# Attention in a two-block network kernel: exponentials ahead of the projection's read-out on ScalarE, the second half of softmax ahead of the joint norms on VectorE, and those norms sooner in layer two

## The chip, the cores and the metric

The kernel runs on one core of a Trainium2 chip. The metric is the device time of one execution in microseconds; the time before is the median of three runs. Five engines work side by side, each through its own list of instructions, in order: TensorE (PE, matrix products and transposes into the eight PSUM banks), VectorE (DVE), ScalarE (ACT), GpSimd (POOL) and SyncE (SP, which issues the weight loads). They are tied together by semaphores written out by hand.

## The reference, cut to what matters

The reference is a two-layer block (attention, spatial gating, a Fourier mixer and a squared-ReLU MLP over 256 latent and 256 context tokens, width 1024) followed by a second block (a gated recurrence, gated linear attention and a mixture of 32 experts). The change touches the attention of the first block alone, of the context in layer one (`context_attention`) and of the latents in both layers (`latent_window_attention`):

```python
s = einsum(q, k) * hd ** -0.5              # 8 heads, 2 kv heads; latents see 256 own + 256 context keys
p = softmax(concatenate([s, s_sink]))      # a learned sink score per head joins each row
out = einsum(p, v)
...
def merge_heads(attn, sgu, four, g_mix, w_out):
    a = rmsnorm(attn, g_mix[:ATTN_WIDTH])                            # "mA"
    s = rmsnorm(sgu, g_mix[ATTN_WIDTH:ATTN_WIDTH + SGU_WIDTH])       # "mS"
    f = rmsnorm(four, g_mix[ATTN_WIDTH + SGU_WIDTH:])                # "mF"
    return jnp.concatenate([a, s, f], axis=-1) @ w_out
```

The three norms of `merge_heads` are the joint norms of this document: mF (Fourier part), mS (gating part) and mA (attention part). Nothing that is computed changes; only the order does.

## The kernel before, in words

X names the latent stream and C the context stream; features lie on partitions and 256 tokens along the free axis. A projection step i (0 to 11) is `w_in(l, s, i)` on TensorE, 16 matmul instructions, and `projected(l, s, i)` on ScalarE, which copies the bank out; steps 6 to 9 go through a GELU, which needs another table of functions than the exponential, so the table is loaded before the GELU and `log_exp()` loads the other one back.

Attention is cut into 8 units: unit u is one pair of heads (one of each kv head, "halves" hf 0 and 1) and one block of 128 queries. A unit runs through these stages:

- `scores` (TensorE, line 572): two products into two neighbouring banks.
- `soft_a` (VectorE, lines 1923 to 1929): for X the band mask, then the maximum, the sink, and the negated maximum, which releases the exponentials (`s_mx`, line 1927).
- `exponentials` (ScalarE, lines 1384 and 1387): two exponentials from the score banks to SBUF, each of which releases its bank, and the sink's.
- `soft_b` (VectorE, lines 1936 to 1940): the sum, its reciprocal, and two products with it, each of which releases (`s_pn`) the transposes of its half.
- `turned` (TensorE, line 580): transposes of the probabilities into two banks. `read_outs` (ScalarE, line 1291) copies those of unit u and the output of unit u-1 out.
- `values` (TensorE, line 594): the product with the values.

TensorE's loop iteration `attention(l, s, i)` issues scores(i+1), turned(i-1) and values(i-2). In layer one the context's attention rides on the latents' projection: step i of it issues `w_in(0, X, i)` and then `attention(0, C, i-2)`. In the latents' attention the filler is pieces of the context's `w_out` (layer one) and rows of the modulation `ada` / `ada_turn` (both layers).

A joint norm goes through all engines: squares on ScalarE, their sum on GpSimd (line 2550), a product with a constant matrix on TensorE (`merge`, that is `mean_summed`, line 478), `mean_read` on VectorE (line 1833), `root` on ScalarE (a logarithm and an exponential, lines 1324 and 1326), `refined` on VectorE (three operations, lines 1838 to 1840) and `scaled` on VectorE (line 1948, one operation per block of 128 features). `value_norm` on VectorE with `value_roots` on ScalarE (lines 1362, 1364) normalises the gating's values before `gating` (line 554).

PSUM banks are handed out in turn by `Fills.take` in the order in which TensorE's code asks; a taker waits until the bank's last user has freed it. So moving one `merge` shifts the bank of everything behind it. The weights go through a ring of three buffers that SyncE refills; in the expert stage it has eight.

Of the kernel before, what the change touches and what calls it, by code (L numbers as in the profile page):

```python
# [14 lines left out]
X, C = 0, 1  # L15
# [102 lines left out]
def build(nc, A, out):  # L118
    (T1, W1), (T2, W2) = smalls()
    ctx = ExitStack()  # L120
    with ctx:
# [299 lines left out]
        def _(pe):  # L421
# [407 lines left out]
            pe.wait_ge(s_kz, 4)  # L829
            scores(1, X, 0)  # L830
            for i in range(10):
                if i == 3:
                    merge("mF", 1, X)
                if i == 5:
                    merge("mS", 1, X)
                attention(1, X, i)
                if 1 <= i <= 4:
                    ada_turn(1, 5 + i)
                if i <= 3:
                    ada(1, 6 + i)  # L840
# [430 lines left out]
        def _(act):  # L1271
# [7 lines left out]
            def freed(key):  # L1279
                b, n, m = F.at[key]  # L1280
                act.wait_ge(s_free[b], n)
# [39 lines left out]
            def root(key, s=0, slot=0):  # L1321

                freed(("ms",) + key)
                S.up(act.activation(stat(s, slot), HOLD[:, 256 * s:256 * s + 256], ACT.Ln))
                act.wait_ge(s_act, S.n)
                act.activation(stat(s, slot), stat(s, slot), ACT.Exp, scale=-0.5).then_inc(s_root, 1)

            def log_exp():
                act.preload_act_table_set("natural_log_exp_and_others")
# [10 lines left out]
            def projected(l, s, i):  # L1340
                key = ("in", l, s, i)
                ks = slice(256 * s, 256 * s + 256)
                if i < 4:
                    evac(Q[s][:, i, :], key)
                elif i == 4 and s == X:
                    evac(KR, key)
                elif i == 4:
                    b = full(key)
                    act.activation(KZ[0:64, 0, ks], banks[b][0:64, 0:256], ACT.Copy)
                    act.activation(KZ[64:128, 1, ks], banks[b][64:128, 0:256], ACT.Copy).then_inc(s_free[b], 1)  # L1350
                elif i == 5:
                    evac(V[:, 2 * s:2 * s + 2, :].rearrange("p a b -> p (a b)"), key)
                elif i < 8:
                    evac(U[s][:, i - 6, :], key, ACT.Gelu_apprx_tanh)
                elif i < 10:
                    evac(GV[s][:, i - 8, :], key, ACT.Gelu_apprx_tanh)
                else:
                    evac(FT[s][:, i - 10, :], key)

            def value_roots(l, s):  # L1360
                act.wait_ge(s_vss, MIX[l, s] + 1)
                S.up(act.activation(SV[:, 32:40], SV[:, 16:24], ACT.Ln))
                act.wait_ge(s_act, S.n)
                act.activation(SV[:, 48:56], SV[:, 32:40], ACT.Exp, scale=-0.5).then_inc(s_vrt, 1)
# [9 lines left out]
            def exponentials(l, s, i):  # L1374
                wd = 512 if s == X else 256
                if i < 8:
                    u, par = units(l, s) + i, i % 2
                    mx, dn, es, nm = (v[:, 2 * par:2 * par + 2] for v in (MX, DN, ES, NM))
                    act.wait_ge(s_mx, u + 1)
                    if i >= 2:  # L1380
                        full(("t", l, s, i - 2, 1))
                    for hf in range(2):
                        b = full(("s", l, s, i, hf))
                        act.activation(P[:, par, hf, 0:wd], banks[b][:, 0:wd], ACT.Exp, bias=mx[:, hf:hf + 1], scale=0.125,
                                       accum_out=dn[:, hf:hf + 1]).then_inc(s_free[b], 1)
                    act.wait_ge(s_es, u + 1)
                    act.activation(es, nm, ACT.Exp).then_inc(s_ex, 1)
# [72 lines left out]
            for i in range(12):  # L1460
# [7 lines left out]
                if i == 9:  # L1468
                    log_exp()
            for i in range(12):  # L1470
                projected(0, X, i)
                if 6 <= i <= 9:
                    log_exp()
                if i == 0:
                    fourier_d(0, C)
                if i == 1:
                    fourier_t(0, C)
                    merge_squares("mF", 0, C)
                    merge_squares("mS", 0, C)
                if i >= 2:  # L1480
                    exponentials(0, C, i - 2)
                if i == 5:
                    root(("mF", 0, C), C, 0)
                if i == 7:
                    root(("mS", 0, C), C, 1)
                if i >= 2:
                    read_outs(0, C, i - 2)
            value_roots(0, X)
            fourier_d(0, X)
            merge_squares("mA", 0, C)  # L1490
            fourier_t(0, X)
# [74 lines left out]
            for i in range(10):  # L1566
                exponentials(1, X, i)
                if 1 <= i <= 4:
                    row(1, 5 + i)
                if i == 3:  # L1570
                    root(("mF", 1, X), X, 0)
                if i == 5:
                    root(("mS", 1, X), X, 1)
                read_outs(1, X, i)
            merge_squares("mA", 1, X)
# [220 lines left out]
        def _(dve):  # L1796
# [18 lines left out]
            def turned(l, c):  # L1815
                b = full(("turn", l, c))
                part = banks[b][:, :].rearrange("p (j g s) -> p j g s", j=4, g=4)
                sums = MODT[:, 192:200].rearrange("p (j s) -> p j s", s=2)
                bias = s1(f"b_ada{l}")[:, 4 * c:4 * c + 4].rearrange("p (j o) -> p j o", o=1).broadcast_to([128, 4, 2])
                if ADA[l, c]:  # L1820
                    dve.wait_ge(s_mod, ADA[l, c])
                dve.tensor_reduce(sums, part[:, :, :, 0:2].rearrange("p j g s -> p j s g"), AX.X, ALU.add).then_inc(s_free[b], 1)
                freed(("turn", l, c))
                dve.tensor_tensor(mod(l)[:, 4 * c:4 * c + 4, :], sums, bias, ALU.add).then_inc(s_mod, 1)
# [6 lines left out]
            def mean_read(key, eps, s=0):  # L1831
                b = full(("ms",) + key)
                dve.tensor_scalar(HOLD[:, 256 * s:256 * s + 256], banks[b][:, 0:256], eps, None, ALU.add).then_inc(s_free[b], 1)  # L1833

            def refined(key, s=0, slot=0):
                r, me, tm = stat(s, slot), HOLD[:, 256 * s:256 * s + 256], HOLD[:, 512 + 256 * s:768 + 256 * s]
                dve.wait_ge(s_root, ROOT[key] + 1)
                step(dve.tensor_tensor(tm, r, r, ALU.mult))
                step(dve.scalar_tensor_tensor(tm, tm, -0.5, me, ALU.mult, ALU.mult))
                step(dve.scalar_tensor_tensor(r, tm, 1.5, r, ALU.add, ALU.mult))  # L1840
                return r
# [259 lines left out]
            for i in range(10):  # L2101
                if i < 8:
                    soft_a(0, X, i)
                if i == 0:
                    mean_read(("mA", 0, C), 1e-6, C)
                if i == 1:
                    refined(("mA", 0, C), C, 2)
                    scaled("mA", 0, C, (0, 1))
                if i == 2:
                    scaled("mA", 0, C, (2, 3))  # L2110
                if 2 <= i <= 3:
                    turned(0, 8 + i)
                if i == 4:
                    gain(0, 3, 5, "g_post_ff", 0.0)
                if i == 3:
                    mean_read(("mF", 0, X), 1e-6, X)
                if i == 4:
                    refined(("mF", 0, X), X, 0)
                if i == 5:
                    scaled("mF", 0, X)  # L2120
                    mean_read(("mS", 0, X), 1e-6, X)
                if i == 6:
                    refined(("mS", 0, X), X, 1)
                if i == 7:
                    scaled("mS", 0, X)
                if 1 <= i < 9:
                    soft_b(0, X, i - 1)
            merge("mA", 0, X)
            post("mix", 0, C)
# [33 lines left out]
            for i in range(10):  # L2163
                if i < 8:
                    soft_a(1, X, i)
                if 2 <= i <= 5:
                    turned(1, 4 + i)
                if i == 3:
                    mean_read(("mF", 1, X), 1e-6, X)
                if i == 4:  # L2170
                    refined(("mF", 1, X), X, 0)
                if i == 5:
                    scaled("mF", 1, X)
                    mean_read(("mS", 1, X), 1e-6, X)
                if i == 6:
                    refined(("mS", 1, X), X, 1)
                if i == 7:
                    scaled("mS", 1, X)
                if 1 <= i < 9:
                    soft_b(1, X, i - 1)  # L2180
            gain(1, 1, 2, "g_post_mix", 0.0)
            gain(1, 2, 4, "g_pre_ff", 1.0)
            merge("mA", 1, X)
# [637 lines left out]
```

## Time and profile before

| | |
|---|---|
| median of three runs | 2383.97 us (2383.86 to 2388.11) |
| profiled execution, its own time | 2384.43 us |
| its span in the trace | 2382.6 us |
| TensorE busy | 2286.0 us, 96% |
| VectorE busy | 811.3 us, 34% |
| ScalarE busy | 489.6 us, 21% |
| GpSimd busy | 145.7 us, 6% |
| layer one: context attention inside the latents' projection | 110 to 180 us |
| layer one: latents' attention | 180 to 240 us |
| layer two: latents' attention | 764 to 811 us |
| expert stage, DMA engines full | from about 1490 us |

A line of the timeline gives the start, how long the group took, the engine, the line of the kernel, the operation, what it writes and reads with shapes, how many instructions were merged, and in brackets how long the engine stood idle just before and what released it. Idle time of TensorE is what counts here; the time of another engine matters only where TensorE waits for it.

### The profile page before, as it was taken

The page shows a single profiled execution, that of the slowest core. Times are in us where ns is not written, and L with a number is a line of the kernel's source. Part 1 is how long each engine was busy: PE and PEld are TensorE (multiplying, and loading weights), DVE is VectorE, ACT ScalarE, POOL GpSimd, SP SyncE. Part 2 cuts the span into 40 slices and gives each one's busy share as a digit, 9 for nine tenths or more (in the row PEclk, how much of TensorE's full clock was granted, in tenths as well). Part 3 has the DMA queues.
Part 4 walks back from the last instruction along what each step waited for, and adds up shares of the span by engine and source line. Part 5 has one row for each costly group of instructions (what it writes and reads, how often), then busy time and mean ns, then how long its engine had stood idle before and what let it go on. Part 6 is the DMA issues. An engine that isn't in the chain of part 4 may idle for free.

```text
span 2382.6 us, 34249 instructions
## 1 busy us (share of the span) xinstructions
PE 2286.0 (96%) x14400; PEld 1672.6 (70%) x14400; DVE 811.3 (34%) x2062; ACT 489.6 (21%) x1153; POOL 145.7 (6%) x150
## 2 busy tenths in 40 slices
PE   6989999999999999999999989999999999999998
PEld 4766888888887678887698855555555555555556
DVE  2245454578434420004674322222222222212224
ACT  3255410000023432101543210111111111111113
POOL 1000211144301000000000000000000000000000
PEclk9999999999999999999999989999999999999999
DMA  8722212134233344345333757999999999999993
GB/s 362 279 106 107 106 71 106 71 129 155 107 141 124 137 172 169 141 145 203 118 131 114 295 235 273 428 426 427 427 426 427 426 426 426 427 427 426 427 426 130
DMA packets 42262, 601.61 MB, mean 252 GB/s; under 512 B 4689, under 2 KB 5329, under 8 KB 5745
## 3 DMA queue, kind: packets, MB, share of 16 engines
q1 hardware_dynamic: 41616, 593.30, 61.4%
q10 hardware_dynamic: 480, 5.97, 0.6%
q8 instruction: 121, 1.98, 0.3%
q14 instruction: 45, 0.36, 0.0%
HBM read 598.20 MB, written 1.05 MB: 252 GB/s over the span
## 4 chain that ended last, share of the span: by engine, by line
PE 85%; DMA 10%; DVE 2%; ACT 2%; issue 1%; POOL 0%; SPq 0%; POOLq 0%; DVEq 0%; PEldq 0%; ACTq 0%
PE PS L1112 15%; PE PS L1136 8%; PE PS L866 8%; PE PS L641 7%; PE PS L676 6%; DMA RG<-in_w_up 6%; PE PS L625 6%; PE PS L728 5%; PE PS L516 4%; PE PS L615 3%; DMA BIG<-in_w_up 3%; PE PS L714 2%; PE PS L1041 2%; PE PS L1148 2%; PE PS L456 1%; PE PS L1107 1%
## 5 line engine op out<-in xcount | busy, mean ns | idle before, releaser
L2410 DVE TENSOR_SCALAR STAT<-PS 128x128 f32<-128x128 f32 (+1 forms) x128 | 37.8, 295 | 669.7 <-PE PS L1112 669.7
L1112 PE MATMUL PS<-BIG,XS 128*64 128x256 f32 (+1 forms) x2016 | 238.8, 388 | 3.3 <-DMA BIG<-in_w_up 3.3
L1112 PEld LDWEIGHTS PS<-BIG,XS 128*64 128x64 f32 (+1 forms) x2016 | 146.5, 139 | 93.8 <-issue 21.4
L1291 ACT ACTIVATE BIG<-PS 128x256 f32<-128x256 f32 (+2 forms) x205 | 85.7, 430 | 499.6 <-PE PS L641 138.9
L1112 PE MATMUL PS<-RG,XS 128*64 128x256 f32 (+1 forms) x1520 | 178.5, 385 | 5.3 <-DMA RG<-in_w_up 5.3
L866 PE MATMUL PS<-XS,RG 128*128 128x256 f32 x768 | 172.8, 383 | 5.0 <-DVE XS L1867 4.1
L866 PEld LDWEIGHTS PS<-XS,RG 128*128 128x128 f32 x768 | 146.3, 192 | 26.7 <-issue 6.9
L1112 PEld LDWEIGHTS PS<-RG,XS 128*64 128x64 f32 (+1 forms) x1520 | 108.3, 138 | 73.7 <-issue 15.6
L1716 ACT ACTIVATE STAT<-STAT 128x128 f32<-128x128 f32 (+1 forms) x128 | 40.1, 313 | 572.8 <-DVE STAT L2410 572.8
L1833 DVE TENSOR_SCALAR HOLD<-PS 128x256 f32<-128x256 f32 x27 | 11.4, 422 | 401.6 <-PE PS L492 301.4
L625 PE MATMUL PS<-HN,RG 128*128 128x256 f32 x640 | 142.0, 385 | 4.0 <-ACT HN L1338 4.0
L625 PEld LDWEIGHTS PS<-HN,RG 128*128 128x128 f32 x640 | 123.5, 193 | 22.0 <-issue 4.6
L1136 PE MATMUL PS<-BIG,CAT 128*64 128x256 f32 (+1 forms) x992 | 121.3, 388 | 0.8 <-DMA BIG<-in_w_down 0.7
L728 PE MATMUL PS<-BIG,RG 128*128 128x256 f32 x512 | 110.7, 379 | 0.0
L516 PE MATMUL PS<-HN,RG 128*128 128x256 f32 x448 | 103.0, 386 | 5.7 <-ACT HN L1338 5.7
L728 PEld LDWEIGHTS PS<-BIG,RG 128*128 128x128 f32 x512 | 97.3, 190 | 13.2
L1136 PEld LDWEIGHTS PS<-BIG,CAT 128*64 128x64 f32 (+1 forms) x992 | 73.4, 139 | 43.8 <-issue 10.0
L516 PEld LDWEIGHTS PS<-HN,RG 128*128 128x128 f32 x448 | 85.1, 193 | 21.6 <-issue 10.0
L2550 POOL TENSOR_TENSOR HN<-HN 128x256 f32<-128x256 f32 x72 | 54.7, 760 | 671.4 <-ACT HN L1319 248.6
L615 PE MATMUL PS<-CAT,RG 128*128 128x256 f32 x384 | 87.1, 386 | 0.2 <-DVE CAT L1948 0.2
L1136 PE MATMUL PS<-RG,CAT 128*64 128x256 f32 x768 | 86.4, 381 | 0.4 <-DVE CAT L2419 0.4
L615 PEld LDWEIGHTS PS<-CAT,RG 128*128 128x128 f32 x384 | 73.2, 192 | 11.7 <-issue 1.0
(353 smaller groups left out, 3286.0 us busy)
## 6 DMA issues: line engine op xcount, KB each, us to landing
BIG<-in_w_up SPq DMA_DIRECT2D x64, 2048.0 KB, 27.1
RG<-in_w_up SPq DMA_DIRECT2D x48, 2048.0 KB, 27.9
RG<-in_w_ff SPq DMA_DIRECT2D x32, 2048.0 KB, 7.7
BIG<-in_w_down SPq DMA_DIRECT2D x32, 2048.0 KB, 29.3
RG<-in_w_ada SPq DMA_DIRECT2D x24, 2048.0 KB, 7.9
RG<-in_w_down SPq DMA_DIRECT2D x24, 2048.0 KB, 28.7
RG<-in_w_in SPq DMA_DIRECT2D x23, 2048.0 KB, 7.9
SM<-in_w_up SPq DMA_DIRECT2D x16, 2048.0 KB, 27.4
```

Source lines behind the costliest of these rows:

```text
L516: m = pe.matmul(banks[b][:, 0:256], w[:, k, c0:c0 + 128], N[:, k, :], start=k == 0, stop=k == 7)
L615: m = pe.matmul(banks[b][:, 0:256], w[:, k, 128 * (n % 4):128 * (n % 4) + 128], own(CAT, s)[:, k, :], start=i == 0, stop=i == 7)
L625: m = pe.matmul(banks[b][:, 0:256], w[:, k, 128 * n:128 * n + 128], own(HN, s)[:, k, :], start=k == 0, stop=k == 7)
L641: m = pe.matmul(banks[b][:, 0:256], w[:, k, :], a[:, k, :], start=not first and k == 0, stop=k == 3, skip_group_check=True)
L676: return pe.matmul(banks[b[j]][:, 256 * half:256 * half + 256], w, a, start=first and half == 0, stop=last, skip_group_check=True)
L714: m = pe.matmul(banks[b[s, o]][:, 0:256], w[:, k, 128 * o:128 * o + 128], own(FFH, s)[:, 16 * h + k, :], start=h + k == 0, stop=h * 16 + k ...
L728: m = pe.matmul(banks[b][:, 0:256], w[:, k, :], own(FFH, s)[:, k, :], start=k == 0, stop=k == 31)
L866: m = pe.matmul(banks[b][:, 0:256], w[:, k, 128 * n:128 * n + 128], src[:, k, 0:256], start=k == 0, stop=k == 7)
L1112: i = pe.matmul(half_of(b, h, sides), Xg[:, k, 0:cap], w[:, k, h * wd:h * wd + wd], start=False, stop=k == 7)
L1136: m = pe.matmul(half_of(b, h, sides), T_[:, k, :], w[:, k, h * wd:h * wd + wd], start=k == 0, stop=k == 7)
L1291: i = act.activation(dst, banks[b][rows, part], fn)
L2550: S.up(pool.tensor_tensor(H[:, i, :], H[:, i, :], H[:, k, :], ALU.add))
```

## The change

Three edits, in four engine programs' order of instructions; none is added or removed.

- ScalarE, layer one, projection of X with the attention of C: in step i the exponentials of unit i-2 come before the projection's read-out and not after it; the root of mF moves from step 5 to step 6 and that of mS from step 7 to step 8, each right behind the exponentials; `value_roots` comes before the read-out of step 11; the reload of the exponential's table moves from right behind the GELU to the end of the step, behind the read-outs.
- VectorE, layer one, attention of X: soft_b of unit 0 comes before `refined` and `scaled` of mA in iteration 1.
- Layer two, attention of X: on TensorE `merge` of mF and mS moves from iterations 3 and 5 to 1 and 2, and with it `root` on ScalarE. On VectorE soft_b comes right behind soft_a, ahead of all norm work, and that moves up: mean_read of mF to iteration 1, refined mF and mean_read mS to 2, refined mS to 3, the two `scaled` to 4 and 5.

```diff
@@ tensor, layer two
             for i in range(10):
-                if i == 3:
+                if i == 1:
                     merge("mF", 1, X)
-                if i == 5:
+                if i == 2:
                     merge("mS", 1, X)
                 attention(1, X, i)
@@ scalar, layer one
             for i in range(12):
+                if i >= 2:
+                    exponentials(0, C, i - 2)
+                if i == 6:
+                    root(("mF", 0, C), C, 0)
+                if i == 8:
+                    root(("mS", 0, C), C, 1)
+                if i == 11:
+                    value_roots(0, X)
                 projected(0, X, i)
-                if 6 <= i <= 9:
-                    log_exp()
                 if i == 0:
                     fourier_d(0, C)
...
                 if i >= 2:
-                    exponentials(0, C, i - 2)
-                if i == 5:
-                    root(("mF", 0, C), C, 0)
-                if i == 7:
-                    root(("mS", 0, C), C, 1)
-                if i >= 2:
                     read_outs(0, C, i - 2)
-            value_roots(0, X)
+                if 6 <= i <= 9:
+                    log_exp()
@@ scalar, layer two
                 exponentials(1, X, i)
...
-                if i == 3:
+                if i == 1:
                     root(("mF", 1, X), X, 0)
-                if i == 5:
+                if i == 2:
                     root(("mS", 1, X), X, 1)
@@ vector, layer one, attention of X
                 if i == 1:
+                    soft_b(0, X, 0)
                     refined(("mA", 0, C), C, 2)
                     scaled("mA", 0, C, (0, 1))
...
-                if 1 <= i < 9:
+                if 2 <= i < 9:
                     soft_b(0, X, i - 1)
@@ vector, layer two, attention of X
             for i in range(10):
                 if i < 8:
                     soft_a(1, X, i)
+                if 1 <= i < 9:
+                    soft_b(1, X, i - 1)
                 if 2 <= i <= 5:
                     turned(1, 4 + i)
+                if i == 1:
+                    mean_read(("mF", 1, X), 1e-6, X)
+                if i == 2:
+                    refined(("mF", 1, X), X, 0)
+                    mean_read(("mS", 1, X), 1e-6, X)
                 if i == 3:
-                    mean_read(("mF", 1, X), 1e-6, X)
+                    refined(("mS", 1, X), X, 1)
                 if i == 4:
-                    refined(("mF", 1, X), X, 0)
+                    scaled("mF", 1, X)
                 if i == 5:
-                    scaled("mF", 1, X)
-                    mean_read(("mS", 1, X), 1e-6, X)
-                if i == 6:
-                    refined(("mS", 1, X), X, 1)
-                if i == 7:
                     scaled("mS", 1, X)
-                if 1 <= i < 9:
-                    soft_b(1, X, i - 1)
```

## Rows read from the trace of the kernel before

**Rows 1.** The page: busy share of the DMA engines in 40 slices of 59.6 us.

```profile
DMA  8722212134233344345333757999999999999993
```

**Rows 2.** Waits of TensorE from 95 to 260 us (total, times, longest).

```profile
PE PS L580 <- ACT BIG L1384: 3.0, 2, 1.5
PE PS L572 <- ACT BIG L1384: 2.2, 2, 2.0
PE PS L594 <- ACT BIG L1384: 1.9, 1, 1.9
```

**Rows 3.** Timeline of TensorE, layer one, projection of X.

```profile
139.93 0.90 PE L580 MATMUL PS<-SM,BIG 128*128 128x128 f32 x4 [1.49 <-ACT BIG L1384]
...
163.71 3.72 PE L516 MATMUL PS<-HN,RG 128*128 128x256 f32 x16
...
175.46 1.09 PE L554 MATMUL PS<-SM,BIG 128*64 128x128 f32 x16 [0.85 <-DVE BIG L1900]
```

**Rows 4.** Timeline of ScalarE, the same stretch.

```profile
131.90 0.42 ACT L1324 ACTIVATE STAT<-HOLD 128x256 f32<-128x256 f32 x1
...
134.27 1.28 ACT L1291 ACT_TABLE_LOAD   x1
...
138.01 1.28 ACT L1329 ACT_TABLE_LOAD   x1
139.31 0.47 ACT L1384 ACTIVATE BIG<-PS,MISC 128x256 f32<-128x256 f32 x1
```

**Rows 5.** Timeline of VectorE, the same stretch.

```profile
135.30 0.17 DVE L1927 TENSOR_SCALAR MISC<-MISC 128x2 f32<-128x2 f32 x1
...
135.59 0.42 DVE L1838 TENSOR_TENSOR HOLD<-STAT 128x256 f32<-128x256 f32 x1
...
137.35 0.62 DVE L1940 TENSOR_SCALAR BIG<-BIG,MISC 128x256 f32<-128x256 f32 x2
```

**Rows 6.** Timeline of VectorE, layer one, attention of X.

```profile
186.75 0.42 DVE L1838 TENSOR_TENSOR HOLD<-STAT 128x256 f32<-128x256 f32 x1
...
189.30 0.88 DVE L1940 TENSOR_SCALAR BIG<-BIG,MISC 128x512 f32<-128x512 f32 x2
...
193.78 0.88 DVE L1940 TENSOR_SCALAR BIG<-BIG,MISC 128x512 f32<-128x512 f32 x2
```

**Rows 7.** Timeline of TensorE, the same stretch.

```profile
189.94 1.06 PE L580 MATMUL PS<-SM,BIG 128*128 128x128 f32 x8 [1.66 <-DVE BIG L1940]
...
195.04 1.04 PE L580 MATMUL PS<-SM,BIG 128*128 128x128 f32 x8
```

**Rows 8.** Waits of TensorE from 690 to 860 us.

```profile
PE PS L580 <- DVE BIG L1940: 2.8, 2, 2.1
```

**Rows 9.** Timeline of VectorE, layer two, end of the attention of X.

```profile
797.67 0.42 DVE L1838 TENSOR_TENSOR HOLD<-STAT 128x256 f32<-128x256 f32 x1
...
799.04 0.16 DVE L1936 TENSOR_TENSOR MISC<-MISC 128x2 f32<-128x2 f32 x1
...
800.24 0.42 DVE L1923 TENSOR_TENSOR PS<-PS,SM 128x256 f32<-128x256 f32 x1
...
802.43 0.87 DVE L1948 SCALAR_TENSOR_TENSOR CAT<-CAT,SM,STAT 128x256 f32<-128x256 f32 x2
```

**Rows 10.** Timeline of TensorE, layer two, attention of X.

```profile
764.54 3.70 PE L572 MATMUL PS<-BIG 128*128 128x512 f32 x8
768.17 1.92 PE L456 MATMUL PS<-RG,SM 128*32 128x512 f32 x16
...
804.24 1.59 PE L580 MATMUL PS<-SM,BIG 128*128 128x128 f32 x8 [2.08 <-DVE BIG L1940]
...
813.62 0.67 PE L478 MATMUL PS<-HN,MISC 128*128 128x256 f32 x2 [2.78 <-POOLq L2553]
```

**Rows 11.** Stretches of TensorE: length, busy (instructions), granted clock, DMA share, GB/s.

```profile
804.00:808.00 4.00, 3.76 (x26) 0.58 0.00 0
859.60:866.40 6.80, 6.53 (x16) 0.52 0.19 82
```

## The prediction, written before the changed kernel was run

> **What bounds the kernel now.** I read the page first. TensorE is busy for 96% of the span, so only its idle time, and time at the lower clock, can be won. In the last third the DMA engines are full [rows 1], but that stage begins when the stages before it have freed their buffers, and TensorE's program gets there in order; so what is won ahead of it should shift it whole. Then the waits of TensorE in the two stretches that the diff touches. From 95 to 260 us three groups wait for line 1384, ScalarE's exponentials, 7.1 us together [rows 2]; in the timeline they are one wait of 1.5 to 2.0 us in each of steps 6 to 9 of the projection, two of them ahead of transposes [rows 3]. Why there: ScalarE's list puts the exponentials behind the step's read-out, that waits for the end of a projection on TensorE, and from step 6 on a table load of 1.28 us follows, and only then the exponentials [rows 4]. The scores' maximum had been there since 135.47 [rows 5], so they come 3.8 us late (139.31), and the transposes' banks are those that they free. Behind it `gating` waits 0.85 us for VectorE's value norm [rows 3], which stood behind `value_roots`.
>
> In the latents' attention of layer one there is one wait, 1.66 us [rows 7]: the first transposes, for a soft_b that stands behind `refined` and `scaled` of mA [rows 6]. In layer two two waits, 2.8 us, for soft_b [rows 8]; the larger stands at 804.24 and behind it TensorE ran near half clock, 1.2 of 2.4 GHz, until 808 [rows 10, 11]. There VectorE is the bound: an iteration costs it 2.2 for soft_a and 1.2 for soft_b (800.24 to 802.43, 799.04 to 800.24) and 0.8 to 1.4 for a piece of a norm (797.67 to 799.04, and line 1948) [rows 9], some 4.4 to 4.8, against 3.9 of TensorE (scores 1.85, half of 3.70 [rows 10], transposes 1.0 [rows 7], values some 1.0). In iterations 0 to 3 the modulation adds over 1.9 to TensorE [rows 10], and VectorE has slack.
>
> **The change, part one: layer one's projection.** Steps 2 to 5 gain next to nothing (0.1), as no wait stands there. I name the steps by their transposes.
>
> Step 6: exponentials at 135.5 and not 139.3; two at 0.47 and the sink's take some 1.1. But the root of mF now stands behind them on ScalarE (0.42 and 0.42 [rows 4], so it ends at 137.45) while `refined` kept its place on VectorE, ahead of soft_b: queued behind the later root are `refined`, soft_b and the transposes. From the start of `refined` to the start of line 1940 is 1.76 [rows 5], its first half some 0.37 and the semaphore some 0.15: 139.74, against 139.93 before. The wait changes hands; with the second half of the transposes, 0.4 won.
>
> Step 7: ScalarE copies out, loads the exponential's table (1.28) and runs the exponentials from 142.6; both banks are free at 143.7, and TensorE, 0.4 earlier, asks at 144.9. The 2.0 us wait goes. Next late is soft_b behind mean_read of mS, 0.4 to 0.5. In all 2.1 won so far.
>
> Step 8 is as step 6, with mS. From the transposes of step 7 (146.35) on: copies out until 147.9, table 1.28, exponentials 1.1, root 0.85, `refined` and soft_b 2.3: 153.4, against 155.63 before. TensorE is there at 152.0 and waits 1.4; 2.4 won so far.
>
> Step 9 has no root: soft_b is done by 156.5, TensorE comes at 158.2, and the bank for the values (scores of unit 7) is free at 156.8. The 1.9 us wait goes whole, and step 10's product starts at 159.3, not 163.71 [rows 3]: 4.4 won. `value_roots` now stands at 164.5, as the squares' sums are there by 161, and the value norm is ready when `gating` asks: 0.9. **Part one: -5.3 us** (7.9 of idle and some 0.6 inside the stretched rows go, 3.2 come back). The GELU's read-outs are now later by up to 1.3, behind a table load, and cover is there: their banks are asked for a step later, some 2 us at least. Bounds: nothing of steps 6 and 8, -4.4; no new wait at all, -8.5.
>
> On the table loads the rows show the next instruction right behind: 138.01 plus 1.28 and the exponential starts at 139.31 [rows 4]. The Trainium skill (ScalarE: Activation LUTs, What ACT_TABLE_LOAD costs) adds a drain of 1380 ns to each switch, 2.66 us in all. The trace does not agree for this kernel; by the page the load of step 7's end, which lies on the path to step 8's transposes, would cost 1.4 more, and with it the sum about 1.4 to 2.8 less.
>
> **Part two: layer one's latents.** soft_b of unit 0 now starts at 186.75, where `refined` stood; it needs some 1.0 to the first release, so 187.8, and TensorE arrives at 188.2. The 1.66 go. But VectorE's work up to soft_b of unit 1 is the same in sum, and its line 1940 stays at 193.78 [rows 6]: with 0.48 for a half and the semaphore, transposes at 194.4, which TensorE could have had at 193.3. Against 195.04 [rows 7] **-0.6 us** is left; behind it TensorE has no wait and all follows it. Bounds: 0 and -1.7.
>
> **Part three: layer two.** `merge` of mF and mS on TensorE is the same some 0.4 each, sooner; GpSimd's sums for both are there before iteration 1. VectorE does the norms in iterations 1 to 5, of which 1 to 3 have slack; in 6 and 7 it has 3.4 against 3.9. What is late next is the tail: unit 7's soft_a can start only when its scores end, and soft_a and soft_b to the first release of unit 6 take 2.2 and 1.0 and 0.15, some 3.4, while TensorE has 2.0 (transposes and values): 1.4 of wait. Gone are 2.8 and 0.2 of wait, 0.2 in stretched rows and half of the 3.76 us at half clock, 1.9 [rows 8, 11]. **-3.7 us.** The 2.78 us behind the last values [rows 10] stay: squares, GpSimd, product. Bounds: if VectorE's backlog only moves, -1; no wait at all, -5.1.
>
> The moved merges shift the banks: scores of units 3, 4 and 5 now take the banks of the scores before them, so a new wait on the exponentials is possible. Unit 3 asks for its second bank at 776.9; the exponentials of unit 2, which have the root of mF and the copies of unit 0's transposes ahead of them, free it at 776.3. Cover 0.6; without it the cost is what is missing, one to one.
>
> Sum: -5.3 - 0.6 - 3.7 = **-9.6 us**. The profiled execution took 2384.43, 0.46 above the median of 2383.97; against the median the forecast is **2374.4 us**.
>
> **The rivals.** (a) *VectorE stays the bound in layer two.* For: it ran without a gap before 804. Against: the count above, 3.4 against 3.9. It would give -1 in place of -3.7, 2377.1. Chance 0.11.
>
> (b) *The clock falls elsewhere.* A fall can take 6.8 us at half rate (859.60 on [rows 11]), 3.4 us lost, and such places stand in the old kernel behind idle TensorE. With the tail's wait still there and the eight matmuls behind it done sooner at full clock, more idle follows in a short time, and a fall could come when work is not waiting anyway: +1.7 to +3.4, 2376.1 to 2377.8. Against: waits of 2.0 and 1.5 us, 7 us apart in layer one, brought no fall. Chance 0.08. By the Trainium skill (TensorE: Matmul & The Clock Gate, What's actually happening) the throttled clock is the default and activity releases it; rows 11 fit that.
>
> (c) *A table load costs more in its new place.* Before, loads followed a copy; now the GELU's follows the exponentials directly and the exponential's a copy. If a switch there held ScalarE for twice its 1.28 [rows 4], the paths to the transposes of steps 7 and 8 would be 1.3 longer each: 2.6 less gain, 2377.0. Against: the exponential in rows 4 starts 0.02 behind its load. Chance 0.03. By the page named above (ScalarE: Activation LUTs, of the Trainium skill) it would be 1.4 each.
>
> (d) *The change does little.* If the new order only swaps the waited-for engine: steps 6 to 8 and layer two keep their waits, only step 9 and gating are won, and 1.9 and 0.9 and 0.6 are left: 2380.6; if the shift is swallowed by weight loads in the DMA-bound stage, 2384. Chance 0.08, mostly within 0.2%.
>
> (e) *Slower: the shifted banks.* If ScalarE's list holds the exponentials of units 2, 3 and 4 behind root and copies for longer than the 0.6 of cover, scores of 3, 4 and 5 wait each. At the price of the worst old wait, 2.1, with a clock fall of 1.7 behind each, that is 11.4, and the old 3.7 are not won: -5.9 + 11.4 = +5.5, 2389.5. It decides when the exponentials of unit 2 end over 0.6 us later than I have them. Against: ScalarE has a quarter of the load there. Chance 0.04.
>
> **How the numbers follow.** The forecast's own case has 0.66 and spans -8 to -12. A measurement of this kernel can tell about 0.2%, 4.8 us, from no change. Forecast, (a), (b) and (c) are all faster by more than that: 0.88. Within 0.2%: 0.08 from (d). Slower: 0.04. The range for 8 in 10 is 2370.8 (step waits smaller than counted, no further fall of the clock) to 2379.0 (bounds of parts one and three at their weak end).
>
> **What would show it.** In the changed profile TensorE's waits for line 1384 in 130 to 165 us should be gone, and two waits of 1.3 to 1.4 us for line 1940 should stand at 138.4 and 152.0, right behind ScalarE's roots; the product of step 10 at about 159.3; no wait ahead of `gating`; the first transposes of the latents without a wait and a new one of about 1 us ahead of the second; in layer two one wait of 1.4 us some 4 us before the last values, no stretch at 0.50 clock ahead of them, and the last `merge` about 9.6 us sooner. A wait of scores (line 572) for line 1384 near layer two's third iteration would show (e) at work. The forecast is wrong if the last `merge` has moved by 9 or more and the total by under 7: then the later stages took it back.

## The result, and the profile after

| | before | changed |
|---|---|---|
| median of five runs each | 2383.86 us (2380.69 to 2388.11) | 2370.30 us (2369.08 to 2372.89) |
| span of the profiled execution | 2382.6 us | 2368.4 us |
| TensorE busy | 2286.0 us | 2277.5 us |

The ratio is 0.9938 (95% interval 0.9922 to 0.9955): times 2383.86 that is 14.8 us less, between 10.7 and 18.6; the medians differ by 13.6. The forecast was 9.6 us less, and the median lies half a microsecond below its range. Faster was right; the size was not, and the question for the experiments is where the other 4 us come from.

First the waits of TensorE in the changed kernel, two lines from 95 to 260 us and two from 690 to 830 us (total, times, longest), against [rows 2, 8]:

```profile
PE PS L580 <- DVE BIG L1941: 4.4, 5, 1.3
PE PS L492 <- ACT HN L1401: 0.5, 1, 0.5
...
PE PS L615 <- DVE CAT L1949: 1.6, 1, 1.6
...
PE PS L580 <- DVE BIG L1941: 1.4, 1, 1.4
```

No wait for line 1384, the exponentials, is left; what remains waits for soft_b (line 1941, one line down from 1940). TensorE's timeline of layer one's projection and of the latents' first steps answers to [rows 3, 7]:

```profile
131.02 0.67 PE L580 MATMUL PS<-SM,BIG 128*128 128x128 f32 x4 [0.40 <-DVE BIG L1941]
...
138.04 0.67 PE L580 MATMUL PS<-SM,BIG 128*128 128x128 f32 x4 [1.24 <-DVE BIG L1941]
...
144.64 0.67 PE L580 MATMUL PS<-SM,BIG 128*128 128x128 f32 x4 [0.40 <-DVE BIG L1941]
...
151.71 0.67 PE L580 MATMUL PS<-SM,BIG 128*128 128x128 f32 x4 [1.29 <-DVE BIG L1941]
...
157.57 3.72 PE L516 MATMUL PS<-HN,RG 128*128 128x256 f32 x16
...
168.41 1.09 PE L554 MATMUL PS<-SM,BIG 128*64 128x128 f32 x16
...
181.06 1.04 PE L580 MATMUL PS<-SM,BIG 128*128 128x128 f32 x8
...
187.36 1.06 PE L580 MATMUL PS<-SM,BIG 128*128 128x128 f32 x8 [1.06 <-DVE BIG L1941]
```

These are the waits that the prediction named: steps 6 and 8 (138.04 and 151.71) wait 1.24 and 1.29 (it had 1.3 and 1.4), step 7 (144.64) waits 0.40, `gating` does not wait, and the latents' wait moved from the first transposes to the second, 1.06. One more, 0.40 at step 5 (131.02), it did not name; counted from `fourier_d` these transposes still come 0.1 us sooner than before. Why steps 6 and 8 still wait is read from ScalarE and VectorE. ScalarE, step 6:

```profile
133.86 0.47 ACT L1384 ACTIVATE BIG<-PS,MISC 128x256 f32<-128x256 f32 x1 [1.26 <-DVE MISC L1928]
...
135.31 0.42 ACT L1326 ACTIVATE STAT<-STAT 128x256 f32<-128x256 f32 x1
135.75 1.28 ACT L1291 ACT_TABLE_LOAD   x1
...
139.64 1.28 ACT L1329 ACT_TABLE_LOAD   x1
140.93 0.47 ACT L1384 ACTIVATE BIG<-PS,MISC 128x256 f32<-128x256 f32 x1
```

VectorE, the same step, against [rows 5]:

```profile
133.86 0.16 DVE L1930 TENSOR_TENSOR MISC<-SM,MISC 128x2 f32<-128x2 f32 x1
135.76 0.43 DVE L1839 TENSOR_TENSOR HOLD<-STAT 128x256 f32<-128x256 f32 x1 [1.74 <-ACT STAT L1326]
...
137.54 0.61 DVE L1941 TENSOR_SCALAR BIG<-BIG,MISC 128x256 f32<-128x256 f32 x2
```

The exponentials run as soon as the maximum is there, but the root now comes behind them, VectorE waits 1.74 us for it with soft_b queued behind, and TensorE waits for soft_b. In ScalarE's lines the exponential starts 0.01 behind the end of its table's load, at its new place too, and the GELU's load starts 0.02 behind the root, so rival (c) fell. The drain that the Trainium skill gives for a switch (ScalarE: Activation LUTs, What ACT_TABLE_LOAD costs) shows in neither trace.

Layer two, TensorE, against [rows 10]:

```profile
756.89 3.70 PE L572 MATMUL PS<-BIG 128*128 128x512 f32 x8
...
794.09 1.06 PE L580 MATMUL PS<-SM,BIG 128*128 128x128 f32 x8 [1.36 <-DVE BIG L1941]
...
797.13 1.99 PE L594 MATMUL PS<-BIG 128*64 128x128 f32 x32
801.91 0.67 PE L478 MATMUL PS<-HN,MISC 128*128 128x256 f32 x2 [2.78 <-POOLq L2555]
802.41 0.59 PE L481 MATMUL PS<-HN,MISC 128*128 128x256 f32 x2
802.85 1.89 PE L615 MATMUL PS<-CAT,RG 128*128 128x256 f32 x8
806.32 26.17 PE L615 MATMUL PS<-CAT,RG 128*128 128x256 f32 x120 [1.58 <-DVE CAT L1949]
```

One wait of 1.36 us is left before the last values, at full clock, as forecast; the wait for GpSimd stays at 2.78. The eight matmuls of w_out behind it now take 1.89 us, at full clock (3.32 before), and the next ones then wait 1.58 for the norm (0.15 before): there the low clock of before had cost almost nothing.

**The ledger.** To see what belongs to the change, I took distances between fixed instructions on TensorE, so that an offset from earlier does not count. Part one runs from the context's `fourier_d` (98.10 after, 99.65 before) to the latents' `gating` (168.41 and 175.46); part two on to the norm mean behind the context's w_out (240.93 and 248.59); part three from layer two's first scores (756.89 and 764.54) to the second product of the last merge (802.41 and 814.13). The ends that are not shown yet, of the changed kernel (98.10, 240.93) and of the kernel before:

```profile
98.10 1.89 PE L531 MATMUL PS<-SM,BIG 128*128 128x256 f32 x8
...
240.93 0.70 PE L492 MATMUL PS<-HN,MISC 128*128 128x256 f32 x2 [0.49 <-ACT HN L1401]
...
99.65 1.89 PE L531 MATMUL PS<-SM,BIG 128*128 128x256 f32 x8
...
248.59 0.70 PE L492 MATMUL PS<-HN,MISC 128*128 128x256 f32 x2 [0.49 <-ACT HN L1401]
...
814.13 0.59 PE L481 MATMUL PS<-HN,MISC 128*128 128x256 f32 x2
```

| us | before | changed | won |
|---|---|---|---|
| start to `fourier_d` | 99.65 | 98.10 | 1.55 |
| part one | 75.81 | 70.31 | 5.50 |
| part two | 73.13 | 72.52 | 0.61 |
| from there to layer two's scores | 515.95 | 515.96 | 0.0 |
| part three | 49.59 | 45.52 | 4.07 |
| the rest to the span's end | 1568.5 | 1566.0 | 2.5 |

The edited stretches give 10.2 us. The other 4 us lie in front of the first moved instruction and behind the last, where the two programs are the same. In front the clock is not the reason, 3.4 us at half clock in both traces; there half of the 1.55 is a wait for weights, 1.15 us before (78.47 us) and 0.37 in the changed kernel (88.80). Behind, the clock differs. Stretches of TensorE around 860 us and behind, of the kernel before, then of the changed one (length, busy, granted clock, DMA share, GB/s):

```profile
844.00:870.00 26.00, 21.42 (x95) 0.87 0.61 243
1074.00:1096.00 22.00, 17.38 (x69) 0.84 0.46 172
1350.00:1392.00 42.00, 38.13 (x194) 0.80 0.57 237
```

```profile
844.00:870.00 26.00, 22.49 (x99) 0.93 0.40 156
1074.00:1096.00 22.00, 19.34 (x82) 0.92 0.74 280
1350.00:1392.00 42.00, 38.68 (x265) 0.88 0.60 247
```

Either this is the chance of one execution (theory 1) or the change shortens the later stages by itself (theory 2).

### The profile page after: what moved, and what is told of

It reads as the page before. It is cut to its first block, busy times and chain, and to the rows that moved or that the text cites. A ratio compares the mean times of both kernels' runs of the same rounds, so it can differ in the third digit from the quotient of the medians.

```text
span 2368.4 us, 34248 instructions
## 1 busy us (share of the span) xinstructions
PE 2277.5 (96%) x14400; PEld 1669.0 (70%) x14400; DVE 810.9 (34%) x2062; ACT 489.8 (21%) x1153; POOL 145.8 (6%) x150
## 4 chain that ended last, share of the span: by engine, by line
PE 84%; DMA 10%; DVE 2%; ACT 2%; issue 1%; POOL 0%; SPq 0%; POOLq 0%; DVEq 0%; PEldq 0%; ACTq 0%
PE PS L1112 16%; PE PS L1136 8%; PE PS L866 8%; PE PS L641 7%; PE PS L676 6%; PE PS L625 6%; PE PS L728 5%; PE PS L516 4%; PE PS L615 3%; DMA BIG<-in_w_up 3%; DMA RG<-in_w_up 3%; PE PS L714 2%; PE PS L1041 2%; PE PS L1148 2%; DMA SM<-in_w_down 2%; DMA RG<-in_w_ada 1%
## 5 line engine op out<-in xcount | busy, mean ns | idle before, releaser
L1112 PEld LDWEIGHTS PS<-RG,XS 128*64 128x64 f32 (+1 forms) x1520 | 108.3, 138 | 73.4 <-issue 15.7
L1834 DVE TENSOR_SCALAR HOLD<-PS 128x256 f32<-128x256 f32 x27 | 11.4, 423 | 393.8 <-PE PS L492 299.8
## 6 DMA issues: line engine op xcount, KB each, us to landing
RG<-in_w_down SPq DMA_DIRECT2D x24, 2048.0 KB, 28.6
```

The source lines that it names most:

```text
L1112: i = pe.matmul(half_of(b, h, sides), Xg[:, k, 0:cap], w[:, k, h * wd:h * wd + wd], start=False, stop=k == 7)
```

## The experiments

Ten runs gave a result, in three groups on three chips, each beside runs of the kernel before on its own chip. The ratios are to those.

**The two kernels once more.** No edit.

> The changed kernel once more. Theory 1 (the three edits are worth what the traces' stretches show, 10.2 us: 5.5 + 0.6 + 4.1, and the rest of the 13.6 between the medians is where TensorE's clock happened to fall): the difference to the kernel before comes out at 10 to 12 us, and the half-clock stretches of this trace differ from those of the first trace of the same kernel by 1.5 to 4 us in sum. Theory 2 (the change itself shortens the later stages, by 2 to 4 us): 13 to 15 us, and the stretches lie as in the first trace.

Measured: 2372.75 us (9 runs, 2368.02 to 2377.95) against 2384.88 (32 runs, 2375.93 to 2391.51), ratio 0.9952 (0.9935 to 0.9968): 11.4 us less, between 7.6 and 15.5.

> The kernel before once more, as a run of its own, so that it has a second trace. Theory 1: the same instructions, yet the stretches of 0.50 granted clock outside the changed part (at 36, 860, 1088, 1371 and 1422 us) differ in length from the first trace; ratio 1.000, within 2 us. Theory 2: they lie as before, to within 0.5 us each.

Measured: 2385.54 us, ratio 1.0006 (0.9993 to 1.0019). But its profiled execution took 2375.7 us of span, 6.9 less than the first trace of the same instructions. The four traces in distances:

| us | before, first | before, second | changed, first | changed, second |
|---|---|---|---|---|
| start to `fourier_d` | 99.65 | 98.73 | 98.10 | 100.79 |
| parts one, two and three, in sum | 198.53 | 198.54 | 188.35 | 188.35 |
| from part two to layer two's scores | 515.95 | 515.99 | 515.96 | 515.97 |
| the rest to the span's end | 1568.5 | 1562.4 | 1566.0 | 1565.8 |
| at half clock, in the whole span | 49 | 32 | 32 | 43 |

Each part is within 0.02 us in the two traces of one kernel. All of the 6.9 lies elsewhere, and on the mean of two traces the rest is no shorter in the changed kernel (1565.9) than before (1565.5). The three stretches of the second trace of the kernel before:

```profile
844.00:870.00 26.00, 21.45 (x102) 0.93 0.60 243
1074.00:1096.00 22.00, 17.37 (x71) 0.92 0.42 150
1350.00:1392.00 42.00, 37.92 (x226) 0.88 0.60 246
```

These are the clocks of the changed kernel's first trace, and the second trace of the changed kernel has those of the kernel before in the first two:

```profile
844.00:870.00 26.00, 22.39 (x89) 0.87 0.35 136
1074.00:1096.00 22.00, 17.38 (x69) 0.84 0.69 266
1350.00:1392.00 42.00, 38.99 (x246) 0.84 0.58 233
```

The table's last row is added up from the granted clock in slices of one microsecond. Half of the 16 us between the two traces of the kernel before is 8, near the 6.0 by which their rests differ. Half of the 10 us between those of the changed kernel is 5, where the spans differ by 2.5: a fall that TensorE would have spent waiting costs less. Theory 2 has nothing left for it in the traces: the later stages change as much between two executions of one kernel as between the kernels.

The times say the same. Each execution's mean granted clock is on record, to 0.001. Of the 60 executions of the kernel before in the three groups, the 13 at 0.993 took 2379.8 us in the mean and the 13 at 0.991 took 2383.6; of the 14 of the changed kernel, the six at 0.993 took 2370.5 and the four at 0.991 took 2372.8. At an equal clock that is 9.3 and 10.8 us less, a coarse measure, as 0.001 of the clock is 4.8 us at half clock; of the 10.2 by distances 1.6 is itself a fall of the clock (priced below), so 8.6 would have been enough. The first five of the changed kernel had a mean clock of 0.9924, its next nine 0.9914, the 60 of before 0.9904; by the 3.8 us between 0.991 and 0.993 the clock accounts for some 3 to 4 us of the first five's lead over the kernel before (an estimate from these means).

**The parts alone.** The diff touches the programs of three engines, not of four. The first of these runs has only the ScalarE hunks of layer one, the second only the hunks of layer two (TensorE, ScalarE, VectorE), the third only `soft_b(0, X, 0)` ahead of the norm.

> The ScalarE edit of layer one alone. Theory 1: 5.4 us less (waits of steps 6 and 8 still 1.2 to 1.3 us each, now for line 1940). If the edits only work together (the third is not independent): under 4. Theory 2 expects 7 or more, as a share of the later stages' gain would come with it.

Measured: 2378.91 us, ratio 0.9972 (0.9957 to 0.9987), 6.7 us less (3.1 to 10.3). Part one is 70.32 us in its trace, 5.49 less than before, parts two and three as before (73.13 and 49.63). The interval of the times holds both what theory 1 and what theory 2 expected; the distances carry this reading. Waits of TensorE from 125 to 262 us: the old 1.66 of the latents is the fifth.

```profile
PE PS L580 <- DVE BIG L1941: 5.0, 5, 1.7
```

> The layer two edits alone. Theory 1: 4.1 us less, and the fall of the clock at 804 us is gone. Rival (VectorE stays the bound in layer two): 1 us less, with the waits for line 1940 still 2.8 us in sum. Theory 2: 6 or more.

Measured: 2379.5 us, ratio 0.9982 (0.9969 to 0.9995), 4.3 us less (1.2 to 7.4). Part three is 46.01 us, 3.6 less than before; 0.5 more than in the changed kernel, with the clock down from 809 us, which takes in its last merge. Up to the first product of that merge it is 45.02 us, as in the changed kernel, against 49.08 before. Part one, where nothing was changed, is 77.46 in this trace and not 75.81: the clock fell at 161 us, behind a wait of 1.9. The time's interval again leaves theory 2's value (6) in. Waits of TensorE from 740 to 858 us:

```profile
PE PS L580 <- DVE BIG L1940: 1.4, 1, 1.4
```

Rival (a), VectorE staying the bound, asked for 2.8 there and fell.

> The VectorE edit of layer one's latents alone, read in the trace. Theory 1: no wait ahead of the first transposes, a new one of 1.0 to 1.1 us ahead of the second, and from the first scores of this attention to the norm mean behind its w_out 0.6 us less. Rival (the soft_b sooner gives its full 1.66 us): 1.7 less and no new wait.

A single execution: part two is 72.53 us, 0.60 less, parts one and three are unchanged, and from 125 to 262 us stands the wait that was expected in place of the 1.66. Its one time, 2387.33 us, is above the median of before and says nothing on 0.6 us.

```profile
PE PS L580 <- DVE BIG L1940: 1.1, 1, 1.1
```

The three parts are independent: 5.49 + 0.60 + 4.06 (up to the last merge) alone, against 10.2 together.

**soft_b first everywhere.** If the waits of steps 6 and 8 only changed hands, soft_b must be taken from behind the norm.

```diff
                 if 2 <= i < 10:
                     soft_a(0, C, i - 2)
+                if 3 <= i < 11:
+                    soft_b(0, C, i - 3)
                 if i == 5:
                     mean_read(("mF", 0, C), 1e-6, C)
...
-                if 3 <= i < 11:
-                    soft_b(0, C, i - 3)
@@ attention of X, layer one
                     soft_a(0, X, i)
+                if 1 <= i < 9:
+                    soft_b(0, X, i - 1)
...
                 if i == 1:
-                    soft_b(0, X, 0)
                     refined(("mA", 0, C), C, 2)
-                    scaled("mA", 0, C, (0, 1))
                 if i == 2:
-                    scaled("mA", 0, C, (2, 3))
+                    scaled("mA", 0, C)
```

> The changed kernel, and on VectorE soft_b ahead of all norm work in both attention loops of layer one too (context: ahead of mean_read, refined and scaled; latents: the scaled of mA behind soft_b of unit 1). Theory 1 (in steps 6 and 8 the wait only changed hands, to soft_b queued behind refined and the later root; likewise 0.4 in steps 5 and 7 and 1.06 at the latents' second transposes): these five waits for line 1941, 4.4 us in sum, go, and nothing of over 0.5 us takes their place; about 14.6 us less than the kernel before. Rival (ScalarE's chain of copies, table load and exponentials is the bound behind them): steps 6 and 8 wait for line 1384 instead, under 2 us won over the changed kernel.

Measured: 2364.52 us, ratio 0.9920 (0.9901 to 0.9939), 19.1 us less than before (14.5 to 23.6). All five waits are gone from 125 to 262 us, and nothing stands in their place:

```profile
PE PS L492 <- ACT HN L1401: 0.5, 1, 0.5
```

VectorE's timeline of step 6 shows soft_b right behind soft_a, and the norm, which nobody waits for, behind it:

```profile
133.87 0.61 DVE L1941 TENSOR_SCALAR BIG<-BIG,MISC 128x256 f32<-128x256 f32 x2
135.30 0.43 DVE L1839 TENSOR_TENSOR HOLD<-STAT 128x256 f32<-128x256 f32 x1 [0.81 <-ACT STAT L1326]
```

Part one falls from 70.31 to 66.04, part two from 72.52 to 71.26: 5.5 us, more than the 4.4 of listed waits. The rival, ScalarE's chain as the next bound, fell. The distances make it 10.2 and 5.5, 15.7 us less than before, near the 14.6 expected; the 19.1 by the times has some clock in it (0.9927 in the mean of these six executions, 0.9899 in the eleven of before).

**Squares sooner.** On top of that, the tail of layer two.

```diff
                 read_outs(1, X, i)
-            merge_squares("mA", 1, X)
+                if i in (3, 5, 7, 9):
+                    merge_squares("mA", 1, X, ((i - 3) // 2,))
```

> As the run before, and in layer two the squares of the attention's parts 0 to 2 are taken inside the loop, as each is ready, so that GpSimd has added them before the last values. Theory 1: of the 2.78 us that the last merge waits for GpSimd some 0.9 is left (copy 0.28, one square 0.42, semaphores), 1.9 won. Rival: the squares sit ahead of exponentials on ScalarE and TensorE waits for those, at most 0.4 each; under 1 won.

TensorE's timeline:

```profile
789.11 1.06 PE L580 MATMUL PS<-SM,BIG 128*128 128x128 f32 x8 [1.29 <-DVE BIG L1942]
...
792.15 2.03 PE L594 MATMUL PS<-BIG 128*64 128x128 f32 x32
794.11 0.70 PE L478 MATMUL PS<-HN,MISC 128*128 128x256 f32 x2
794.99 0.70 PE L481 MATMUL PS<-HN,MISC 128*128 128x256 f32 x2 [0.18 <-ACT HN L1319]
```

The 2.78 us wait is gone, where some 0.9 had been expected to stay, and part three is 43.29, another 2.23 less, by the distance; the wait for the norm behind it is unchanged (1.59). The times don't show it: 2366.88 us, ratio 0.9932 (0.9915 to 0.9950), above the kernel without it, in six runs each, at a mean clock of 0.9908 against 0.9927. Two microseconds drown in this spread.

**Filled waits.** If falls of the clock behind TensorE's long waits make the spread, TensorE should be kept busy in them. The changed kernel, with products of a constant tile into a bank that is overwritten next:

```diff
+            def warmed(b, count):
+                for _ in range(count):
+                    pe.matmul(banks[b][:, 0:256], ones, onet, start=True, stop=True)
...
@@ w_in, before the waits of (0, C, 0)
+                        warmed(b, 8)
@@ ff1, layer two, first tile
+                    warmed(b, 7)
@@ lin2, first tile
+                    warmed(b, 8)
```

> The changed kernel, and TensorE runs 8, 7 and 8 products that nothing reads, of ones into the bank that it overwrites next, in its three waits of 3.5 to 4.2 us (ahead of the context's projection in layer one, of the MLP in layer two, and of the second block's projection). They add 23 products to the work, inside waits. Theory 1 (the falls at 34, 847 and 1076 us come from these waits and cost half of their 3.4 to 6.8 us each): these three are gone or come elsewhere less often, 4 to 6 us less than the changed kernel. Theory 2 (the clock has nothing to do with it): no difference, or 0.5 us more.

Measured: 2361.42 us, ratio 0.9915 (0.9896 to 0.9934), 20.3 us less than before (15.7 to 24.8), some 10 more than the change alone, where 4 to 6 were expected. In the three filled waits the clock is full:

```profile
30.00:36.00 6.00, 4.58 (x31) 1.00 1.01 426
844.00:849.40 5.40, 5.02 (x24) 1.00 1.00 428
1070.00:1080.00 10.00, 8.79 (x34) 1.00 0.57 210
```

> The kernel before with the filled waits alone. Theory 1 (the falls behind the three long waits are a thing apart from the change): 4 to 8 us less than before, like the changed kernel's; the falls at 804 and 814 us, behind layer two's attention, stay. If the falls depended on the new order: no gain here.

The same edit in the kernel before: 2377.66 us, ratio 0.9966 (0.9950 to 0.9982), 8.1 us less (4.3 to 11.9). So it is worth about the same without the change. Two of the three filled waits show no fall. The first does: there TensorE waited 1.54 us for weights before the added products, and they themselves ran at half clock:

```profile
34.00:35.00 1.00, 1.00 (x4) 0.50 1.11 475
```

One part of the expectation failed: the falls at 804 and 814 us did not stay; in this trace there is one at 156 us and none there, though the 2.1 us wait stands as before. A wait invites a fall but does not fix it. This trace also prices the falls: without the one at 804 part three is 48.04 us, 1.55 less than with it (49.59), and with the one at 156 part one is 77.50, 1.69 more than without (75.81).

**All together.** The change, soft_b first, the squares sooner and the filled waits.

> The changed kernel with all three further edits: soft_b first in layer one, the squares sooner in layer two, the products that fill TensorE's three long waits. Theory 1: 10.2 (the change) + 5.5 (soft_b first) + 2.2 (squares) + some 6 (clock) = about 24 us less than the kernel before, ratio 0.990; no fall of the clock in the three filled waits.

Measured: 2353.48 us (2352.54 to 2360.73), ratio 0.9880 (0.9862 to 0.9898), 28.6 us less than before (24.3 to 32.9), where about 24 were expected. None of the three filled waits shows a fall. Its trace spent 10 us at half clock, 3.4 of them at the very end, where TensorE has stopped.

## Why the prediction was right and wrong

- **What bounds.** Right. The waits of steps 6 to 9 were the read-out and the table load ahead of the exponentials, and moving them removed all four waits for line 1384; the part alone is worth what the whole shows there.
- **Part one**, -5.3 forecast, 5.50 measured in two traces each and by the part alone. The wait that changes hands at steps 6 and 8 came at 1.24 and 1.29; soft_b first removed it. What the sum had too small is the stretched rows: 7.9 of idle went and 3.3 came back, as counted, and the rows gave 0.9 in place of 0.6. Step 10's product moved from 163.71 [rows 3] to 157.57, by 6.14, of which 1.55 were there from the start: 4.6, where 4.4 was forecast.
- **Part two**, -0.6, measured 0.61, with the new wait of 1.06 that gives the rest of 1.66 back.
- **Part three**, -3.7, measured 4.07. The new wait was 1.36, as worked out. The term was 0.4 too small, by two errors of opposite sign. The fall of the clock was worth 1.55 (part three with and without it) and not 1.9: its row has 3.76 us busy at 0.58, not at 0.50, which makes 1.6. The short waits inside rows that show no idle time gave some 0.9 where I had 0.2 (4.07 less 1.55 of clock and less 1.64 of listed waits, of which 3.00 went and 1.36 came).
- **Bank shift**, rival (e): no wait for scores appeared. There was cover enough.
- **Sum**: 9.6 forecast, 10.2 shown. That step stands.
- **What failed** is the step from the sum to the measured time, "against the median the forecast is 2374.4", and the range built around it. It took the difference of two medians to be the difference of two programs. The kernel before alone spans 2375.93 to 2391.51 us in 32 runs, and two single executions of it differ by 6.9 us outside the edited stretches, 6.0 behind them, mostly by the clock, and 0.9 ahead. Rival (b) saw the mechanism, but only as a loss at one place, with 0.08; in fact outside the edited stretches the clock falls in six or seven places of either kernel, and what it takes there differs each time, both ways. At rival (b)'s own place, behind the last merge, a fall came in the second trace of the changed kernel (805 to 810 us) and cost 0.1 us, as the wait for the norm took it up. The range's slow end was also not what it says: parts one and three at their weak ends, -4.4 and -1, with -0.6 give 2378.0 and not 2379.0. The sentence that a measurement can tell 0.2% was too sure as well: the first interval was 0.33% wide, and the second, with more runs, is centred on 11.4 us. Both intervals of the changed kernel hold 10.7 to 15.5 us in common, and the first does not hold 10.2, by half a microsecond.

That the first 4 us were mostly chance of those ten executions is shown by the rest of the span, which is no shorter in the changed kernel on the mean of two traces, by the 9 to 11 us at an equal clock, and by the difference going smaller with more runs (11.4). A share of about a microsecond stays open: the new order may change how often the clock falls. Against falls in layer one the prediction had that its waits of 1.5 to 2.0 us brought none; of five traces with these waits two have a fall there that cost 1.7 us (at 161 and at 156 us), and of seven with the new order none has one, which are too few to say how much it is worth.

## What to carry to other kernels

Where an engine's list mixes a chain that another engine waits for with work that nobody waits for yet, put the chain first on every engine at once: here moving it on ScalarE alone left 5.5 us behind a norm on VectorE, which a short move there then gave. Judge an edit of a few microseconds by distances between fixed instructions of the trace, and not by the whole time, which spread over 15 us in one program. The distances repeated to 0.02 us here where the clock was the same in them; one fall inside added 1.7, so look at the granted clock of the stretch first.

## What the runs showed of the hardware that I had not expected

The granted clock of TensorE fell to 0.50 (1.2 of 2.4 GHz) for 3.4 or 6.8 us at the same wait in different executions of the same kernel: behind 858 us 3.4 in one trace and 6.8 in the other. Filling three waits of 3.5 to 4.2 us with 23 products that nothing reads took 8.1 us (4.3 to 11.9) off the kernel before. By the Trainium skill (TensorE: Matmul & The Clock Gate, What's actually happening) the throttled clock is the default and activity releases it. The traces agree for eight of the nine filled waits, which ran at 1.00; the ninth fell to 0.50 with the products running, behind a wait of 1.54 us for weights. The fall at 804 us, which the prediction counted as a sure gain of 1.9 us, was in four of the five traces that have the waits ahead of it and not in the fifth, the one with filled waits, so even that term had chance in it.

The clock is not all of the spread. The start of `fourier_d`, behind the same instructions in the nine traces without filled waits, lay between 96.81 and 103.14 us; the latest had waited 3.00 us for weights at 80 us and had a fall of the clock behind it.
